# Two transformer blocks in one program: quadrant-wise inverse, the overflow step inside the experts' block, one block for the last norms, and moved loads and projections

## The reference

```python
h = h + rms_norm(mix, post_mix_norm[i])       # mix: RWKV7, sparse attention (NSA), S5; @ w_out
f = conv_ffn(rms_norm(h, pre_ffn_norm[i]), w_up[i], conv_w[i], conv_b[i], w_down[i])
h = h + rms_norm(f, post_ffn_norm[i])
e = rms_norm(p[i] @ w_ple[i], ple_norm[i])
gate = jax.nn.sigmoid((h @ w_ple_gate[i]).astype(jnp.float32)).astype(h.dtype)
h = h + gate * e
```

## Time and profile before

| what | us |
|---|---|
| median of 3 runs (range) | 2658.7 (2658.69 to 2658.9) |
| profiled execution: its own time | 2656.14 |
| its span | 2653.8 |
| up to the last expert's second wave | 1819.4 |
| from there to the end of the scan's work (2296.2) | 476.8 |
| SP alone, to the next block | 15.5 |
| the two norms before the FFN | 24.10 |
| conv FFN | 233.10 |
| tail, from 2568.9 | 84.90 |

### The profile page before, as it was taken

How to read it: one execution, slowest core, us unless ns; L and a number is a source line. 1 busy time by engine, 2 the same in 40 slices (tenths; PEclk the granted TensorE clock), 3 DMA queues, 4 the chain that set the end, 5 groups by cost and what they waited for, 6 DMA issues and landing times. The chain is left out here.

```text
span 2653.8 us, 44248 instructions
## 1 busy us (share of the span) xinstructions
PE 2447.3 (92%) x20113; PEld 1668.8 (63%) x20113; DVE 607.3 (23%) x1305; ACT 303.6 (11%) x609; POOL 144.7 (5%) x196
## 2 busy tenths in 40 slices
PE   7999989998999989999999999999769898589976
PEld 6677778886777754443535445353458786478865
DVE  1432310002432311010101101010143426333332
ACT  0222200000221111000000000000023112100000
POOL 1000000000000000000000000000040353000000
PEclk8999989998999979999999999999879557889988
DMA  7322524344222539999999999999532000423320
GB/s 277 127 80 67 195 72 173 129 159 162 95 80 80 190 136 341 389 384 376 410 370 411 370 391 394 372 412 370 209 87 97 0 1 9 187 70 130 137 83 16
DMA packets 165241, 533.56 MB, mean 201 GB/s; under 512 B 16028, under 2 KB 31295, under 8 KB 148671
## 3 DMA queue, kind: packets, MB, share of 16 engines
q1 hardware_dynamic: 158960, 529.86, 52.9%
q10 hardware_dynamic: 6094, 0.88, 0.2%
HBM read 529.67 MB, written 1.05 MB: 200 GB/s over the span
## 5 line engine op out<-in xcount | busy, mean ns | idle before, releaser
L182 PE MATMUL bank<-hT,ring 128*128 128x256 f32 x3280 | 745.5, 387 | 18.0 <-PEq L479 14.4
L182 PEld LDWEIGHTS bank<-hT,ring 128*128 128x128 f32 x3280 | 631.4, 194 | 118.6 <-issue 29.7
L182 PE MATMUL bank<-ring,moe_he 128*32 128x512 f32 (+1 forms) x6144 | 579.6, 539 | 0.4 <-DVE moe_he L1624 0.4
L182 PEld LDWEIGHTS bank<-ring,moe_he 128*32 128x32 f32 x6144 | 199.2, 110 | 375.8 <-issue 373.9
L182 PE MATMUL bank<-ring,moe_actT 128*32 128x256 f32 x5376 | 293.0, 379 | 0.0
L182 PEld LDWEIGHTS bank<-ring,moe_actT 128*32 128x32 f32 x5376 | 174.6, 110 | 117.2 <-issue 3.4
L1675 DVE TENSOR_TENSOR moe_act<-moe_silu,bank 128x512 f32<-128x512 f32 (+1 forms) x48 | 26.9, 617 | 540.6 <-PE bank L182 540.6
L182 PE MATMUL bank<-cffn_act,ring 128*128 128x256 f32 x352 | 79.7, 379 | 0.4 <-DVE cffn_act L1285 0.4
L182 PE MATMUL bank<-ffn_act,ring 128*128 128x256 f32 x352 | 79.4, 379 | 0.0
L182 PEld LDWEIGHTS bank<-cffn_act,ring 128*128 128x128 f32 x352 | 66.8, 190 | 9.8 <-DVE cffn_act L1285 0.8
L182 PEld LDWEIGHTS bank<-ffn_act,ring 128*128 128x128 f32 x352 | 66.9, 190 | 9.1
(11 more groups left out here) (617 smaller groups left out, 1999.1 us busy)
## 6 DMA issues: line engine op xcount, KB each, us to landing
ring<-in_moe_w_down SPq DMA_DIRECT2D x56, 2048.0 KB, 13.7
ring<-in_moe_w_gate SPq DMA_DIRECT2D x32, 2048.0 KB, 16.6
ring<-in_moe_w_up SPq DMA_DIRECT2D x32, 2048.0 KB, 10.6
ring<-in_w_in SPq DMA_DIRECT2D x29, 2048.0 KB, 8.4
ring<-in_moe_w_gate SPq DMA_DIRECT2D x32, 1536.0 KB, 7.9
ring<-in_moe_w_up SPq DMA_DIRECT2D x32, 1536.0 KB, 8.3
ring<-in_w_up SPq DMA_DIRECT2D x10, 2048.0 KB, 9.8
ring<-in_w_out SPq DMA_DIRECT2D x6, 2048.0 KB, 7.8
```

The source lines that it names most:

```text
L182: ins = pe.matmul(out, lhsT, rhs, start=start, stop=stop, **kw)
```

## The change

- **Experts**: the last expert's second wave has 11 hidden blocks for 12. The overflow loop stands in the experts' block. Its first step now computes the last expert's last hidden block, for the rows that the expert took. SP issues the loads before the second block's, waits until the last activations are turned, runs the loop's loads, and issues the rest.
- **Masks** of 64 columns for each half, in place of 128x128.
- **Projections** without S5; `state_input` makes its two features at the end of rounds one and three of `attend`.
- **Inverse** on diagonal quadrants: each matrix of 128 is done as two of 64x64, rows and columns 0 to 63 and 64 to 127 in turn, with 32 moving columns. X, XT, LT and PP have 768 elements a partition for 1536. XT is built on DVE; LM has two buffers, and POOL is two levels ahead. The products of the opening are those of L2434's form, and two heads' scores stand before the transposes.
- **Loads**: in the scan SP issues only up to the second load of the conv FFN, two more in each of the two norms.
- **End**: `last_norms`, one block for the norm after the FFN, the embedding, its norm, the gates, and the output. The gates' first half runs by k as each part of `xT` comes; the second half by output tile, with sigmoid, product, sum and transposes of a tile behind it.

```diff
+LAST_BLOCK = D_FFE // P - 1
+
+
+def waves(e):
+
+    return WAVES if e < N_EXPERTS - 1 else (WAVES[0], (16, 11))
...
-                k.step(g_.memset(x.spread[:, :, N_EXPERTS, :], 0.0))
                 k.step(g_.memset(x.stepf[:], 0.0))
                 k.step(g_.memset(x.stepf[:, 0:1], float(N_EXPERTS)))
+                k.step(g_.memset(x.stepf[:, N_STEPS:N_STEPS + 1], float(N_EXPERTS - 1)))
+                k.step(g_.memset(x.stepf[:, 2 * N_STEPS:2 * N_STEPS + 1], float(LAST_BLOCK)))
...
+            with pe.Fori(0, count(pe)) as i:
+                pe.wait_ge(w_in.sem, i * 48 + 48)
...
+                v.tensor_scalar(x.spread[:, 0, N_EXPERTS, :], x.spread[:, 0, N_EXPERTS - 1, :], -1.0, float(2 * CAP - 1),
+                                ALU.mult, ALU.add)
+                v.tensor_copy(x.spread[:, 1, N_EXPERTS, :], x.spread[:, 1, N_EXPERTS - 1, :])
...
+            m.issue(sp, m.number[("2", "kv")])
+            m.clear_last(sp)
+            sp.wait_ge(at_ready.sem, half * N_EXPERTS)
+            sp.sem_inc(step_added.sem, 1)
+            with sp.Fori(0, count(sp)) as i:
...
-             ("swap_w", 1), ("gates", 9), ("s5", 2), ("turned", 3))
+             ("swap_w", 1), ("gates", 9), ("turned", 3))
...
+                        k.step(g.tensor_tensor(self.levels[h], blocks[h, 1:7, c], blocks[h, 0:6, c], ALU.subtract))
+                        k.step(g.tensor_tensor(self.low0[h, :], self.levels[h, 0, :], self.low[h, c], ALU.mult))
...
-                    feature("s5", 0)
...
-        LT, X = (slot(2, 1536 * i, 12, P) for i in range(2))
-        XT, PP = (slot(3, 1536 * i, 12, P) for i in range(2))
+        LT, X, XT, PP = (slot(2, 768 * i, 12, CHUNK) for i in range(4))
...
-        LM = m.hT[:, 0:6, :].rearrange("p k n -> p (k n)").rearrange("p (a n) -> p a n", a=12)
-        rounds = slot(2, 3072, 2, T)
+        self.KT, self.QB, self.QK = slot(2, 3072, 12, CHUNK), slot(4, 0, 12, CHUNK), slot(4, 768, 12, CHUNK)
+        LM = [slot(3, 2048 + 768 * i, 12, CHUNK) for i in range(2)]
...
+                    def state_input(j):
+
+                        w = m.slab(pe, ("2", "s5"))
+                        for k in range(KD):
+                            m.mm(pe, m.bank[6][:, 0:T], w[:, k, j * P:(j + 1) * P], m.hT[:, k, :], k == 0, k == KD - 1,
+                                 u_ready if k == KD - 1 else None)
+                        if j == 1:
+                            m.done_with_slab()
+
                     def blocks(n, bank0, lhsT, rhs, part):
                         w = 2 ** n
                         for i in range(12):
-                            x = rhs[:, i, :].rearrange("p (b u w) -> p b u w", u=2, w=w)[:, :, part, :]
-                            o = m.bank[bank0 + i // 6][:, i % 6 * 64:(i % 6 + 1) * 64].rearrange("p (b w) -> p b w", w=w)
-                            ins = pe.matmul(o, lhsT[:, i, :], x, start=True, stop=True)
+                            for c in range(2):
+                                x = rhs[R2[c], i, :].rearrange("p (b u w) -> p b u w", u=2, w=w)[:, :, part, :]
+                                o = m.bank[bank0 + c][R2[c], i * 32:(i + 1) * 32].rearrange("p (b w) -> p b w", w=w)
+                                ins = pe.matmul(o, lhsT[R2[c], i, :], x, start=True, stop=True)
                         return ins
...
+                    products(self.beta, self.alpha, 4)
+                    products(self.alpha, self.beta, 6)
+                    scores(0)
+                    scores(1)
...
+                            p_ready.on(blocks(n, 4, LM[(n - 1) % 2], X, 0))
...
+                            pe.wait_ge(u_out.sem, n // 2)
                             dx_ready.on(blocks(n, 6, XT, PP, 0))
...
+                        if n in (1, 3):
+                            pe.wait_ge(x_out.sem, 2 * n)
+                            state_input(n // 2)
...
+                    masked(LT, 0, 4, self.strict)
+                    masked(X, 1, 6, self.low0)
+                    v.wait_ge(mat_out.sem, 4)
                     soften(0)
+                    v.tensor_tensor(X, X, compact(self.unit, 12), ALU.add)
+                    k.step(v.tensor_tensor(XT, LT, compact(self.up0, 12), ALU.mult))
+                    k.step(v.tensor_tensor(XT, XT, compact(self.unit, 12), ALU.add), x_in)
...
+                            for c in range(2):
+                                xs = first(X[R2[c]], w)
+                                x_out.on(v.tensor_tensor(xs, xs, out_of(6 + c, R2[c], w), ALU.subtract))
...
+                    for n in range(1, LEVELS + 1):
+                        if n > 2:
+                            angles(2 * n - 6)
+                            angles(2 * n - 5)
+                            g.wait_ge(p_ready.sem, n - 2)
+                        lm_ready.on(g.tensor_tensor(LM[(n - 1) % 2], LT, compact(self.levels[:, n, :], 12), ALU.mult))
...
                     sp.dma_start(self.wglu, m.a["s5_w_glu_2"][0].rearrange("(k p) n -> p k n", p=P)).then_inc(m.load_in[3], 16)
+                    m.ahead = m.number[("2g", 0)] + 2
                     m.prefetch(sp)
...
+    m.ahead += 2
+    rmsnorm(m, m.xT[:], m.hT, "pre_ffn_norm_2", extra=load_ple)
+    m.ahead = 10 ** 6
...
+    ORDER = (0, 2, 1, 3, 4, 6, 5, 7)
...
+                pe.wait_ge(sq_ready.sem, 1)
+                sums(sq, 0, sum_ready)
+                pe.wait_ge(pT_in.sem, 1)
+                embed(0)
+                embed(1)
+                pe.wait_ge(wide_ready.sem, 1)
+                spread.on(pe.matmul(m.bank[6][:, 0:T], m.ones[:], w1[:], start=True, stop=True))
+                embed(2)
+                embed(3)
+                for k in range(4):
+                    pe.wait_ge(x_ready.sem, k + 1)
+                    for n in range(KD):
+                        gate(n, k)
+                    if k == 2:
+                        pe.wait_ge(sq_ready.sem, 2)
+                        sums(g, T // 4, sum_ready)
+                    if k == 3:
+                        pe.wait_ge(wide_ready.sem, 2)
+                        spread.on(pe.matmul(m.bank[5][:, 0:T], m.ones[:], w2[:], start=True, stop=True))
+                pe.wait_ge(x_ready.sem, KD)
+                for i, n in enumerate(ORDER):
+                    if n % 2:
+                        pe.wait_ge(sig_ready.sem, ORDER.index(n - 1) + 1)
+                    for k in range(4, KD):
+                        gate(n, k)
+                    if i >= 2:
+                        turn(ORDER[i - 2])
+                turn(ORDER[-2])
+                turn(ORDER[-1])
...
+                for i, n in enumerate(ORDER):
+                    act.wait_ge(gate_ready.sem, i + 1)
+                    act.activation(g[:, n, :], m.bank[n // 2][:, n % 2 * T:(n % 2 + 1) * T], ACT.Sigmoid).then_inc(sig_ready.sem, 1)
...
+                    k_.step(v.tensor_tensor(e[:, n, :], e[:, n, :], g[:, n, :], ALU.mult))
+                    v.tensor_tensor(e[:, n, :], e[:, n, :], m.xT[:, n, :], ALU.add).then_inc(out_ready.sem, 1)
...
         if stop > 4:
+            m.ahead += 2
             rmsnorm(m, m.hT[:], None, "post_mix_norm_2", add_to=m.xT)
         if stop > 5:
+            m.ple_in = m.sb("ple_in", [P, TT, PLE])
             conv_ffn(m)
-            ple(m)
-        finish(m)
-
-
-def finish(m):
-
-    nc, a = m.nc, m.a
-    with ExitStack() as ctx:
-        y = m.sb("y_out", [P, TT, D], ctx=ctx)
-        turned, copied, stored = m.signals(3)
-        with nc.Block() as block:
-            @block.tensor
-            def _(pe):
-                for j in range(TT * KD):
-                    t, k = divmod(j, KD)
-                    pe.transpose(m.bank[j // 4][:, (j % 4) * P:(j % 4 + 1) * P], m.xT[:, k, t * P:(t + 1) * P],
-                                 m.ident[:]).then_inc(turned.sem, 1)
-
-            @block.vector
-            def _(v):
-                for q in range(4):
-                    v.wait_ge(turned.sem, 4 * q + 4)
-                    v.tensor_copy(y[:, q // 2, (q % 2) * 512:(q % 2 + 1) * 512], m.bank[q][:]).then_inc(copied.sem, 1)
-
-            @block.sync
-            def _(sp):
-                out = a["out"][0].rearrange("(t p) d -> p t d", p=P)
-                for t in range(TT):
-                    sp.wait_ge(copied.sem, 2 * t + 2)
-                    sp.dma_start(out[:, t, :], y[:, t, :]).then_inc(stored.sem, 16)
-                sp.wait_ge(stored.sem, 16 * TT)
-        m.end_block()
+            last_norms(m)
```

More of the change, by code:

```diff
@@ L1614, in _ @@
             act.activation(x.ye[:, 0:2, :], DN[0][:].rearrange("p (g n) -> p g n", g=2), ACT.Copy).then_inc(ye_ready.sem, 1)
+            with act.Fori(0, count(act)) as i:
+                act.wait_ge(pair_ready.sem, i + 1)
+                act.activation(x.most, m.bank[4][:, 0:T], ACT.Silu).then_inc(sig_ready.sem, 1)
         @block.vector
@@ L3013, in ple @@
[L3013 to L3024 removed]
+                k_ = Engine(v, vchain.sem)
```

335 lines of the change are left out of this document (168 added, 167 removed).

## The result

The changed kernel takes 2534.9 us (median of 4 runs, 2528.2 to 2540.1) against 2658.7: a ratio of 0.9535, with a 95% interval of 0.9512 to 0.9558. The prediction was 2553, range 2514 to 2580. The profiled execution has a span of 2533.0 for 2653.8, so 120.8 us went.

The account below looks back on a forecast made before the run. TensorE was taken as busy up to the last expert, with four later stretches not bound by their work; terms there summed to -105.9 us from 2656.1, 2550.2, plus 2.6 to the median: 2553, range 2514 to 2580.

Parts of the forecast that it names:

- heads and inverse: Stage between projections and scan: quadrant products, S5, switches, clock and opening together -36.6 us, a stretch of 104 us.
- rival (b): Heads and inverse: the clock rises and stays, the stretch takes 66 us, 38 less, so 2515 in all; chance 0.13.
- The quadrant product: Inverse: 48 quadrant instructions at 53 ns, 2.56 us for 5.33; over 14 products -38.8 us.
- Rival (c): Inverse: quadrants take turns at 107 ns each, +36 us, so 2589; chance 0.08.
- Switches: Inverse: one more change between full and quadrant tiles at each of 14 products, 0.33 us each, +4.6 us.
- The clock behind the S5 projections: Heads and inverse: wide S5 products lift the clock and the next few products run at it, -6 us (0 to -10).
- The opening: Start of heads and inverse, 18.6 us: smaller masks, X and XT, quadrant products; about 12 us, -6.6 (0 to -10).
- Experts: Last expert and overflow step: one hidden block fewer, loads issued earlier, warm products; -17.0 us (bounds -12 and -20).
- Scan's end: End of the scan's block: SP issues two loads instead of six, -15.3 us (-5 if the norms are held).
- Rival (d): Norms behind the scan: loads moved from the scan hold them, the 15.3 us stays, so 2568; chance 0.07.
- Tail: From the norm after the FFN to the end: seven blocks become one, 51.4 us for 84.9, -33.5 (-27 to -38).
- Rival (e): Inverse: an instruction costs 223 ns whatever its size, +114 us, so 2667, slower; chance 0.02.

## Why the prediction was right, and where its terms were off

**Direction and range** held, and so did the mechanism of every part. The forecast was 18 us too slow. Of that 12.7 is one stretch, heads and inverse; 2.6 is the step from the profiled time to the median, which this time are equal. The range was wide, 66 us, because it took in rival (b).

**The quadrant product.** Taken at 53 ns an instruction at half clock; measured 56 (2.70 us from the start of one product of 48 to what follows it). The chosen neighbour was the right one, and the reading "two quadrants work side by side" is borne out by the run that put them one after the other: 101 ns, with the bank changing along. Rival (c) was thus a true hazard of the form of the loop, though not of the change.

**Switches.** +4.6 was put down. PE's weight loads ahead of the 14 products wait 2.7 us in all for nothing the profile shows, so about 0.2 each where 0.33 was taken; with all products at half clock (S5 back in the projections) it is 4.3 us, 0.31 each. The sum of cold rounds is the better test: predicted 74.4 + 4.6 = 79.0 for five rounds; with no wide work in them they lasted from 2056.4 to about 2135.2, 78.8. The two small terms were right together.

**The clock behind the S5 projections** was the step that failed: "the next few products run at it: -6 (0 to -10)". By the measured parts it is 78.8 + 10.85 (both projections) less 72.9 (2052.6 to 2125.6), so -17, outside my bounds. I had the mechanism and its sign from two groups of 16 in the projections, and took it for a matter of a few products; it lasted for nine, and what is fast in a round is also its transposes, values and scores (a round of 9.5 us for 16.2). Rival (b), "the clock rises and stays", had its share here: 9 of 14 products. It came nearest with wide work in each round, 10 to 13 of 14 and a stage of 79.2 to 87.3 us, not its 66. The Trainium skill (*TensorE: Matmul & The Clock Gate*, Part 1) has the throttled clock as the default state, which activity releases. The trace agrees in part: without wide work in the rounds PE was busy 76.91 of 78.80 us and the granted clock stayed at 0.50, while behind the S5 projections it was 0.99 and 0.98.

**The opening** took 9.2 us for 12: the two groups of quadrant products took 2.8 us for the 7.6 of the 24 products before, and VectorE's masks 2.0 for 4.5, each less than half. PE still waits there 3.2 us for VectorE's second operation on XT.

**Experts.** -19.5 for -17.0: 1.1 us between scatter and step for 2.2, and an earlier start of the last contraction by 4.0 us, not 2.6. Part of the 1.4 us between 4.0 and 2.6 is luck: over the twelve profiles with the joined block, final_norm starts at 1904.5 to 1907.0, so the term is -17.3 to -19.8. What I did not see is that a block's semaphores are cleared by SP in the next block, behind its loads. The joined block has 26 for 7; final_norm, which had SP as its last engine, grew by 1.6 us. Moving the clears gave 1.4 back there, and 3 us went in the projections.

**Scan's end** -14.8 for -15.3, and +15.1 when undone: shown. Rival (d) did not come; the norms took 24.4 us for 24.1.

**Projections, masks**: -3.0 for -2.5 and -0.4 for -1. The projections' 3.0 hang on the clock of one group: where it ran at half clock, the same projections took 108.5 us, as many as before the change.

**Tail** -36.3 for -33.5. The end was as worked out: 2.6 us from the last gate (2527.3) to the end of the last copy (2529.84) for about 2.9, and 3.16 from there for 3.15. PE came to the end of its last gate 2.5 us sooner, 42.9 us into the stage for 45.4: the second sums and the spreads cost 1.9 for 2.9, the transposes between the gates 1.1 for 2, and the embedding, most of it at full clock, 8.1 for 8.96.

**Rival (e)**, 223 ns an instruction, is out: 32 to 56 ns.

## What to carry to other kernels

A stage of small matmuls can be bound by the clock that it keeps PE at, not by their number: look at the granted clock of the stage, and where it is 0.50 with PE busy, put wide work that is due anyway between the small work. Four pieces in place of two groups made more products fast in every profile, but that the kernel got faster by it alone is not shown. Small products on diagonal quadrants paid here only with neighbouring instructions on different quadrants (and banks); the order of two loops was worth 42 us. And a block ends with its slowest queue: loads issued into a full queue belong where another engine is at work. Moving the clearing of semaphores paid in its own block and not in the whole, as a group behind it then ran at half clock.

## What the runs showed of the hardware

- Wide work lifted the clock whatever it was for: products of 64x64 tiles with PE busy nearly throughout ran at 2.77 us for 48 (half clock), and behind 16 instructions in a row of 128x128 weights with 128 or 256 columns at 1.59. 64 unread instructions saved some 16 us. Wide weights alone did not do it: the rounds of before, 128x128 weights with 64 columns, stayed at 0.50.
- How long the clock stays up varies with the execution: four programs that are the same up to the end of the heads' stage took 84.8, 84.8, 91.1 and 91.2 us for it; two with the same stage behind another start took 92.9 and 93.0. A single run of such a kernel says little about a few us: one version with the four pieces took 2518 once, another, which also moved the clears, 2527 to 2533 in five runs.
- Two quadrants in turn, each with its own bank: 56 ns an instruction against 101 one after the other at half clock, 32 against 56 at full.
- 26 semaphores cleared on SP made a block 15.9 to 16.5 us long that took 14.8 to 15.1 with 7 there or with none: some 1.3 us, about two of SP's small DMA issues in it (0.5 to 0.6 us each).
